# Turning the differential keys through VectorE's squares and DRAM, and moving their scores

## The reference

```python
proj = jnp.einsum('bsd,dn->bsn', rms_norm(x, pre_w, NORM_EPS), w_in)
dq, dk, dv, dg, sq, sk, sv, sg, iq, ik, iw = jnp.split(proj, SPLIT_OFFSETS, axis=-1)
dq = apply_rope(dq.reshape(b, s, DIFF_HEADS, 2, DIFF_QK_DIM), cos_d, sin_d)
dk = apply_rope(dk.reshape(b, s, DIFF_HEADS, 2, DIFF_QK_DIM), cos_d, sin_d)
# differential attention, causal:
p = softmax(einsum('bqhcd,bkhcd->bhcqk', dq, dk) * scale)
oa = einsum('bhqk,bkhe->bqhe', p[:, :, 0] - lam * p[:, :, 1], dv)
# sparse attention: top 64 causal keys of sum_h relu(iq_h . ik) * iw_h
ob = softmax(einsum(sq, sk_chosen) * scale) @ sv_chosen
mix = concatenate([rms_norm(oa, subln_w) * (1 - lambda_init) * silu(dg), ob * silu(sg)])
out = x + rms_norm(mix @ w_out, post_w)
```

## Time and profile before

| | |
|---|---|
| Median of 3 runs | 300.79 us (300.02 to 301.07) |
| The profiled execution | 299.94 us, its span 298.1 us |
| TensorE matmuls | 291.0 us (98%) |
| TensorE weight loads | 245.5 us (82%) |
| VectorE | 235.9 us (79%) |
| ScalarE | 163.9 us (55%) |
| GpSimd | 70.1 us (24%) |
| DMA | 61.05 MB, 205 GB/s over the span |
| Granted TensorE clock | 0.994 of full |

### The profile page before, as it was taken

One profiled execution on the slowest core, in us unless ns is written; L12 is line 12 of the kernel. 1 busy time (PEld: TensorE's weight loads), 2 busy tenths in 40 slices (PEclk: granted clock), 3 DMA queues, 4 the chain that ended last, 5 costly groups with the idle time before them and its releaser, 6 DMA issues.

```text
span 298.1 us, 4395 instructions
## 1 busy us (share of the span) xinstructions
PE 291.0 (98%) x1560; PEld 245.5 (82%) x1560; DVE 235.9 (79%) x476; ACT 163.9 (55%) x284; POOL 70.1 (24%) x116
## 2 busy tenths in 40 slices
PE   8999999999999999999999999999999999999992
PEld 7799778788787888888888988778888788888892
DVE  4853989889999996966984686978999999878543
ACT  5976863736577473803665854473737756391101
POOL 6548510203030311101070740002303030310101
PEclk9999999999999999999999999999999999999997
DMA  7999959467528669981059799937644684746012
GB/s 262 373 369 386 366 217 347 133 158 222 184 89 184 239 178 286 253 243 48 0 158 372 245 350 243 305 143 202 219 141 143 117 305 146 183 86 154 1 70 70
DMA packets 66741, 61.05 MB, mean 205 GB/s; under 512 B 38816, under 2 KB 43680, under 8 KB 66720
## 3 DMA queue, kind: packets, MB, share of 16 engines
q1 hardware_dynamic: 66432, 60.52, 65.0%
q10 hardware_dynamic: 288, 0.26, 0.3%
HBM read 55.01 MB, written 5.77 MB: 204 GB/s over the span
## 4 chain that ended last, share of the span: by engine, by line
PE 94%; DMA 2%; SPq 1%; ACT 0%; DVE 0%; issue 0%; POOLq 0%; DVEq 0%; POOL 0%; ACTq 0%
PE bank_a L469 20%; PE bank_a L478 20%; PE bank_a L474 20%; PE bank_a L626 7%; PE bank_s L626 6%; PE bank_o L603 4%; PE bank_t L448 3%; DMA w_raw<-in_w_in 2%; PE bank_a L486 2%; PE bank_s L587 2%; PE bank_s L579 1%; PE bank_s L567 1%; PE bank_t L626 1%; PE bank_o L474 1%; PE bank_s L474 1%; PE bank_o L478 1%
## 5 line engine op out<-in xcount | busy, mean ns | idle before, releaser
L994 DVE TENSOR_TENSOR w_lo<-w_raw,w_hi 128x2048 fp32r<-128x2048 f32 (+1 forms) x46 | 98.5, 2147 | 17.9 <-ACT w_hi L770 17.6
L770 ACT ACTIVATE w_hi<-w_raw 128x2048 fp32r<-128x2048 f32 (+1 forms) x46 | 81.9, 1785 | 31.5 <-PE bank_a L478 23.3
L469 PE MATMUL bank_a<-w_hi,h_hi 128*128 128x512 f32 (+1 forms) x272 | 72.4, 388 | 0.0
L478 PE MATMUL bank_a<-w_lo,h_hi 128*128 128x512 f32 (+1 forms) x272 | 70.0, 379 | 0.0
L474 PE MATMUL bank_a<-w_hi,h_lo 128*128 128x512 f32 (+1 forms) x272 | 69.9, 379 | 0.0
L478 PEld LDWEIGHTS bank_a<-w_lo,h_hi 128*128 128x128 f32 x272 | 49.6, 188 | 10.1 <-DVE w_lo L994 0.7
L474 PEld LDWEIGHTS bank_a<-w_hi,h_lo 128*128 128x128 f32 x272 | 49.8, 188 | 9.8
L469 PEld LDWEIGHTS bank_a<-w_hi,h_hi 128*128 128x128 f32 x272 | 48.0, 188 | 10.4 <-issue 2.7
L838 ACT ACTIVATE xt_pbuf<-xt_pbuf,st 128x128 f32<-128x128 f32 (+1 forms) x48 | 21.3, 444 | 25.1 <-DVE st L1143 25.1
L1437 POOL TENSOR_TENSOR rt<-nat,tab 128x256 f32<-128x256 f32 x10 | 7.4, 740 | 112.2 <-ACT nat L822 112.1
L822 ACT ACTIVATE nat<-bank_a,st 128x512 f32<-128x512 f32 x20 | 13.5, 681 | 19.6 <-PE bank_a L478 19.6
(11 more groups left out here) (199 smaller groups left out, 430.8 us busy)
## 6 DMA issues: line engine op xcount, KB each, us to landing
w_raw<-in_w_in SPq DMA_DIRECT2D x30, 1024.0 KB, 5.9
w_raw<-in_w_out SPq DMA_DIRECT2D x8, 1024.0 KB, 6.0
w_raw<-in_w_in SPq DMA_DIRECT2D x8, 584.0 KB, 7.4
turned<-mixn SPq DMA_DIRECT2D x20, 128.0 KB, 2.7
prm<-in_rows SPq DMA_DIRECT2D x2, 705.0 KB, 6.9
w_raw<-in_w_in SPq DMA_DIRECT2D x2, 512.0 KB, 6.4
xres<-in_x SPq DMA_DIRECT2D x2, 512.0 KB, 9.9
dqT<-turned SPq DMA_DIRECT2D x2, 512.0 KB, 5.9
```

The lines of the kernel that those rows point to most:

```text
L469: pe.matmul(bank, h_hi[:, HALF * half + kk, tok], whi[:, kk, :], start=half == 0 and kk == 0, stop=False)
L478: mm = pe.matmul(bank, h_hi[:, HALF * half + kk, tok], wlo[:, kk, :], start=False, stop=half == 1 and kk == HALF - 1)
L770: act.activation(unit(w_hi, u), unit(raw, u), ACT.Copy).then_inc(hi_done.sem, 1)
L994: dve.tensor_tensor(unit(w_lo, u), unit(raw, u), unit(w_hi, u).bitcast(F32), ALU.subtract).then_inc(lo_done.sem, 1)
```

## The change

Differential keys take the way through VectorE's squares and DRAM as the queries do. TensorE's eight transposes and VectorE's two copies a layer go; a turning of squares, four puts and two readings come, with semaphores dk_squares, dk_put and dk_landed and one more DRAM buffer. The scores 6 to 9 stand half a chunk later in TensorE's list, behind second(14), and 10 and 11 behind second(15). The turnings of probabilities and VectorE's and ScalarE's lists are arranged around that. The copy of the index keys stands ahead of split_lo(9) in layer 0. On SP some readings and puts stand one weight unit earlier (index queries, PS1, the mixture), and the parameters' reading two units later.

```diff
-T_IK, T_DK, T_PD0, T_PD1A, T_SK, T_PD1B = 4, 5, 7, 8, 9, 11
+T_IK, T_PD0, T_PD1A, T_SK, T_PD1B = 4, 5, 6, 7, 9
...
@@ SP
                     if layer and u == 8:
                         sp.wait_ge(iq_squares, 1)
                         put(0, squares, iq_put)
-                    if layer and u == 9:
                         sp.wait_ge(iq_put, 16 * SQUARES)
                         get(0, iqT, iq_landed)
...
+                    if u == 14:
+                        sp.wait_ge(dk_squares.sem, dk_squares.at(layer, 1))
+                        put(DKS, squares, dk_put.sem)
+                        sp.wait_ge(dk_put.sem, dk_put.at(layer, 16 * SQUARES))
+                        for b in range(BLOCKS):
+                            sp.dma_start(dkT[:, :, b * P:(b + 1) * P], scratch[DKS][:, b * HEADS:(b + 1) * HEADS, :]).then_inc(dk_landed.sem, 16)
...
-                    if layer == 0 and u == 1:
+                    if layer == 0 and u == 3:
                         sp.dma_start(prm[:, :], rows[0:1, :].to_broadcast([P, ROW_N])).then_inc(prm_landed.sem, 16)
...
                     if u == 1:
                         get_probs(layer, PS0)
-                    if u == 2:
                         put_probs(layer, PS1)
...
                         get_probs(layer, PS1)
-                    if u == 3:
+                    if u == 2:
                         sp.wait_ge(mix_put.sem, mix_put.at(layer, 16 * SQUARES))
@@ TensorE
-                turn_nat(T_DK, 0, 3)
                 first(13)
-
-                pe.wait_ge(t_drained.sem, t_drained.at(layer, T_DK + 2))
-                pe.wait_ge(dq_landed.sem, dq_landed.at(layer, dq_landed.per_layer))
-                diff_scores(6, 0, range(HEADS))
-                diff_scores(8, 1, (0, 1))
                 second(13)
                 first(14)
                 second(14)
+
+                pe.wait_ge(dq_landed.sem, dq_landed.at(layer, dq_landed.per_layer))
+                pe.wait_ge(dk_landed.sem, dk_landed.at(layer, dk_landed.per_layer))
+                diff_scores(6, 0, range(HEADS))
+                diff_scores(8, 1, (0, 1))
                 first(15)
+                second(15)
+                diff_scores(10, 1, (2, 3))
+                first(16)
 
                 pe.wait_ge(combined.sem, combined.at(layer, 1))
                 turn_probs(T_PD0, 6, 0, HEADS)
-                diff_scores(10, 1, (2, 3))
-                second(15)
 
                 pe.wait_ge(combined.sem, combined.at(layer, 2))
                 turn_probs(T_PD1A, 8, 1, 2)
-                first(16)
                 second(16)
                 turn_nat(T_SK, 0, 5)
                 first(17)
 
-                pe.wait_ge(combined.sem, combined.at(layer, 3))
-                turn_probs(T_PD1B, 10, 1, 2)
-
                 pe.wait_ge(t_drained.sem, t_drained.at(layer, T_SK + 2))
                 pe.wait_ge(sq_landed.sem, sq_landed.at(layer, sq_landed.per_layer))
                 dsa_scores(12, 0, range(HEADS))
+
+                pe.wait_ge(combined.sem, combined.at(layer, 3))
+                turn_probs(T_PD1B, 10, 1, 2)
@@ ScalarE
                 split_hi(layer, 16)
+                move(13)
+                move(14)
                 exps(6, 0, 4)
                 exps(7, 0, 4)
-                move(13)
                 split_hi(layer, 17)
                 exps(8, 1, 2)
                 exps(9, 1, 2)
-                move(14)
+                move(15)
                 split_hi(layer, 18)
                 exps(10, 1, 2)
                 exps(11, 1, 2)
-                move(15)
@@ VectorE
+                if layer == 0:
+                    drain(T_IK, ikT[:, :])
                 split_lo(layer, 9)
-                drain(T_IK, ikT[:, :])
+                if layer:
+                    drain(T_IK, ikT[:, :])
...
                 mask_unchosen(0)
+                dve.wait_ge(dq_put.sem, dq_put.at(layer, 16 * SQUARES))
+                turn_squares(0, 3, dk_squares.sem)
                 split_lo(layer, 14)
 
-                choose(1, 1)
-                drain_pair(T_DK, dkT)
+                choose(1, 3)
+                split_lo(layer, 15)
                 choose(1, 2)
-                split_lo(layer, 15)
+                split_lo(layer, 16)
                 mask_scores(6, 0, 4, causal[:, P:SEQ])
                 mask_scores(7, 0, 4, causal[:, P:SEQ])
-                choose(1, 2)
+                mask_scores(8, 1, 2, causal[:, :])
+                mask_scores(9, 1, 2, causal[:, :])
...
                 combine(6, 0, HEADS, 0)
 
-                mask_scores(8, 1, 2, causal[:, :])
-                mask_scores(9, 1, 2, causal[:, :])
-                dve.wait_ge(dq_put.sem, dq_put.at(layer, 16 * SQUARES))
+                dve.wait_ge(dk_put.sem, dk_put.at(layer, 16 * SQUARES))
                 turn_squares(1, 4, sq_squares.sem)
-                split_lo(layer, 16)
                 combine(8, 1, 2, 0)
-
+                split_lo(layer, 17)
+                choose(1, 2)
                 drain(T_PD0, pT[:, 0, :])
                 mask_scores(10, 1, 2, causal[:, :])
                 mask_scores(11, 1, 2, causal[:, :])
-                split_lo(layer, 17)
-                choose(1, 2)
                 drain(T_PD1A, pT[:, 1, :])
+                choose(1, 1)
+                drain_pair(T_SK, skT)
                 combine(10, 1, 2, 2)
-                choose(1, 1)
+                split_lo(layer, 18)
+                mask_scores(12, 0, 4, work[0][:, :])
+                drain(T_PD1B, pT[:, 2, :])
                 mask_unchosen(1)
-                drain_pair(T_SK, skT)
-                split_lo(layer, 18)
-
-                drain(T_PD1B, pT[:, 2, :])
-                mask_scores(12, 0, 4, work[0][:, :])
+                turn_probs(PS0, 12)
                 split_lo(layer, 19)
-                turn_probs(PS0, 12)
-                split_lo(layer, 20)
-
-                gate_diff(0)
-                split_lo(layer, 21)
                 mask_scores(13, 1, 2, work[1][:, :])
                 mask_scores(14, 1, 2, work[1][:, :])
 
+                gate_diff(0)
+                split_lo(layer, 20)
                 turn_probs(PS1, 14)
                 dve.wait_ge(subln_ready.sem, subln_ready.at(layer, 1))
-                drain_mix(T_MD0, m_hi, m_lo, 0, subln)
                 gate_diff(1)
                 turn_mix()
+                drain_mix(T_MD0, m_hi, m_lo, 0, subln)
+                split_lo(layer, 21)
```

More of the change, by code:

```diff
@@ L86 @@
 ROW_N = sum(ROW.values())
-T_IK, T_DK, T_PD0, T_PD1A, T_SK, T_PD1B = 4, 5, 7, 8, 9, 11
-T_MD0, T_MS0, T_MS1 = 12, 13, 14
-T_USES = 15
-PS0, MD1S, PS1 = range(3, 6)
+T_IK, T_PD0, T_PD1A, T_SK, T_PD1B = 4, 5, 6, 7, 9
+T_MD0, T_MS0, T_MS1 = 10, 11, 12
+T_USES = 13
+DKS, PS0, MD1S, PS1 = range(3, 7)
 LANES = 32
@@ L236, in build_trunk @@
         iq_squares, iq_landed = sem("iq_squares"), sem("iq_landed")
+        dk_squares, dk_put, dk_landed = count("dk_squares", 1), count("dk_put", 16 * SQUARES), count("dk_landed", 16 * BLOCKS)
         dq_squares, sq_squares = count("dq_squares", 1), count("sq_squares", 1)
@@ L820, in move @@
                         act.wait_ge(dq_squares.sem, dq_squares.at(layer, 1))
+                    if chunk == SK:
+                        act.wait_ge(dk_squares.sem, dk_squares.at(layer, 1))
                     root = {DQ: rd, SQ: rs}.get(chunk, rx)
```

## The result

The changed kernel takes 304.49 us (median of 6 runs, 304.13 to 305.90) beside 300.42 us for the kernel before (6 runs, 299.95 to 301.07): a ratio of 1.0141, 95% interval 1.0117 to 1.0165. It is slower by 4.1 us. Two later runs in a slower state, one of the kernel before (367.93 us) and one of the third experiment (979.17 us), are in none of the medians. The profiled execution took 304.84 us, its span 303.1 us, 5.0 more than the 298.1 of before.

A forecast was written before the change was run, and what follows sets the result against it. TensorE's back-to-back list was taken as the bound: 299.94 + 2 x (2.6 - 0.97) - 0.2 + 0.1 = 303.1 us profiled; from the runs' median, 300.79 + 3.2 = 304.0 us, range 301.2 to 307.2.

The forecast's parts named there:

- TensorE's list: TensorE's sequence of work: without the eight differential-key transposes it is 0.97 us a layer ahead if nothing makes it wait.
- The wait at SK: Value-key transposes wait for VectorE's copies of PD0 and PD1A: 2.6 us a layer, about 1.1 and 1.5.
- The one loose term: Ahead of PD1A's copy, one VectorE product and split_lo(17) each wait for GpSimd's rotary work: 1.0 us, bounds 0 and 2.4.
- Rival 1: No wait at SK, PD1A being copied before 99.33: 298.7 us, chance 0.1.
- all 14.5 us of VectorE's work: VectorE's work between the first mask and PD1A's copy, without a wait; TensorE is there 14.5 us later.
- What is late next: With the wait for PD1A gone, the drain of SK behind it would still come late; no size given.
- The keys through DRAM: Differential keys' readings, issued at 77.1 and 77.5, land between 80 and 83.4, taken as 81.5, needed at 83.67: no wait.
- The opening: Parameters' reading behind unit 7 lets units 6 and 7 land up to 2 us earlier: 0.2 us gained, bounds 0 and 0.5.
- PS0: Layer 0: reading of PS0's probabilities comes behind the next layer's unit 0: 0.1 us added, bounds 0 and 0.5.
- rival 5: TensorE's clock falls to 1.2 GHz in the new pause: 2.7 us more a layer, 309 us, chance 0.05.
- the base: Starting time of the forecast: median of the runs, 300.79 us, with the profiled execution 0.85 below it.

The follow-up runs named there:

- third experiment: Changed kernel with GpSimd's rope of the value-side keys SK left out but for one head's columns of one block: 301.3 us, ratio 1.0034.
- reordered kernel: Changed kernel with only VectorE's list rearranged: copies of PD0 and PD1A behind split_lo(17), two rounds of choose moved behind PD1B's copy: 298.75 us, ratio 0.9951.
- last one: Reordered kernel with the reading of PS0's probabilities directly behind their puts, ahead of the next layer's unit 0: 298.75 us.
- first experiment: Changed kernel with VectorE's copies of PD0 and PD1A right behind split_lo(17), ahead of two rounds of choose and masks 10 and 11: 301.94 us, ratio 1.0060.
- second experiment: The run of the reordered kernel, against the changed kernel: 298.75 us, ratio 0.9951.
- late reading alone: Kernel before with only the parameters' reading moved behind unit 7 in layer 0: 299.85 us, ratio 0.9989.
- pause filled: Changed kernel with unread 512-column matmuls, three ahead of the first four value-key transposes and four ahead of the second four: 302.94 us, ratio 1.0087.
- fifth kernel: Changed kernel with the parameters' reading put back behind unit 5: 305.32 us (303.91 to 306.48, 5 runs).

## Why the prediction came out right, and where only the sum did

**TensorE's list**: 0.97 us a layer predicted, 0.92 measured, in layer 1 of the reordered kernel and in layer 0 of the last one. Eight transposes and one interruption, nothing hidden.

**The wait at SK**: mechanism, place and size are as walked. In layer 0, with the predicted value in brackets: from the first mask (84.71) to combine(6) 4.27 us (4.27); combine(8) starts at 92.7 (92.8); PD1A's copy ends at 101.6 (101.9); waits of 1.10 and 1.47 (1.1 and 1.5). The one loose term was GpSimd, at 0.74 for 1.0, inside the bounds of 0 and 2.4. Two of VectorE's instructions met it, as supposed, but neither was held for a whole one of GpSimd's: the products took 0.49 more and the low half 0.26. In the changed kernel no mask and no bank copy ran beside the rope of SK. Elsewhere copies did, untouched: in before PD1A's copy took 0.69 us beside GpSimd's last instruction (98.77 to 99.51, its usual 0.74), and in the first experiment both copies together took 1.27 us beside the rope and 1.29 for a pair away from it.

The Trainium skill (GPSIMD Engine Reference, Key points) has GpSimd contend with VectorE's instructions that have two SBUF inputs or run in a two-port mode, and the copies fit that. No mask ran beside the rope in any of the kept traces, so of the masks they show nothing.

**Rival 1** rested on the sentence that "even an ideal order only breaks even". That holds only as long as all 14.5 us of VectorE's work stay ahead of the copy. The second experiment puts some of it behind, and both copies are out at 98.4, before TensorE asks (98.78). So the wait was a choice of order.

**What is late next**: said of the case without the wait for PD1A, and shown by the first experiment: the drain of SK, 1.56 us late.

**The keys through DRAM**: their readings were issued at 76.90 (77.1 predicted) and landed 3.2 us later, as the page's list of DMA issues has it:

```profile
dkT<-turned SPq DMA_DIRECT2D x4, 256.0 KB, 3.2
```

They were in at about 80.5, 3 us ahead of the scores: the early end of my range, and not the 81.5 that I took. The rule of the Trainium skill on 512-byte pieces (DMA: Bandwidth & Descriptors, Specifications) had pointed to that end, and the trace agrees.

**The opening**: 0.2 us predicted, bounds 0 and 0.5; 0.4 measured, with the late reading alone and from before to after (18.68 to 18.28). The mechanism is right (ScalarE's high copies of units 6 and 7 start 1.7 and 2.1 us earlier in after), the term was too small. I took a part of the weight loads' waits of 0.7 us; more than half of them came back, and without the late reading a low half that is just in time in before is late in the changed kernel.

**PS0**: 0.1 us predicted in layer 0, and 0.1 lost there. It is no more because the pause has made TensorE late itself; with the pause gone it loses 0.5 (second experiment). The cover was the very wait that I had added elsewhere.

**The clock, rival 5**: this is the step that failed. I gave it 0.05 and argued that pauses of 1.1 and 1.5 us are shorter than the 2 us after the last matmul in the earlier trace rows. That took one row for a limit, and took the two pauses one by one, though TensorE works only 0.41 us between them. In the profiled execution the clock fell in one layer of two. The other executions can be read by their mean granted clock. With the pause filled it is 0.995 to 0.998. Of after's six, five have 0.992 or 0.993, and the slowest (305.90 us) 0.986. Of the fifth kernel's five, the fastest (303.91) has 0.996, three (305.19 to 305.36) 0.990 to 0.992, and the slowest (306.48) 0.987. Steps of 1.1 to 1.4 us are near what no fall, one and two would give. So I take it that the clock falls in one of the layers in most executions and in none or both in some; only the two profiled ones, with one fall each, show it in a timeline. I had priced it at 2.7 a layer, a whole half group more; it lasts 3.4 us in which TensorE works on at half speed, and costs 1.6.

**The total**: 304.0 forecast, 304.49 measured, and the closeness is partly luck. With the clock kept the changed kernel takes 302.9, so my sum without the clock was about 1.1 too high. Of that, 0.4 to 0.5 is the base: I had added the 0.85 us between the profiled execution and the median of three (300.79), and more runs put that median at 300.4 and 300.2. The opening gave 0.2 more than I allowed. The other 0.4 or so stays open; medians of 4 to 6 runs don't settle it. The clock, which the sum left out, took 1.55. The sign doesn't hang on it: with the clock kept the ratio is 1.0087, still slower.

## What to carry to other kernels

When an edit renumbers or moves the users of a shared buffer, ask for each of them whose release it waits for, and what stands ahead of that release on the other engine. Here the change shortened the busy engine's list by 1.8 us and lost 5.1 at a bank whose copy stood behind selection and masks that nobody was waiting for; with those moved behind the copies the same change gains 1.5. A pause of the matmul engine is priced twice, once for its length and once for the clock that it may cost.

## What the runs showed of the hardware

- TensorE's granted clock fell to 0.50 at the end of a pause of 1.1 and 1.5 us with four transposes between. In the fifth kernel it fell 0.9 us after TensorE had gone on (at 103.2, the pause over at 102.3), again for 3.4 us. It did so in one layer of the two in both profiled executions; what decides it, no run shows. In the eight executions with one wait of about 1.5 us and a short one of 0.4 a layer (first and third experiments) the mean clock is 0.994 to 0.998, so that no such loss is seen. After the last matmul it held for about 2.0 us in before, and for about 4 in after (columns as in the earlier trace rows):

```profile
297.00:298.00 1.00, 0.43 (x4) 0.22 (x2) 0.03 (x1) 0.47 (x2) 0.00 (x0) 1.00 0.00 0
...
300.00:301.00 1.00, 0.00 (x0) 0.00 (x0) 0.57 (x2) 0.00 (x0) 0.00 (x0) 1.00 0.37 139
301.00:302.00 1.00, 0.00 (x0) 0.00 (x0) 0.00 (x0) 0.00 (x0) 0.00 (x0) 0.77 0.99 346
```

So one row at the end of a trace is no limit for what a pause may be.

- Where GpSimd's rope ran beside VectorE's products and low halves, both lost time in places, and not evenly. Of the rope of SK beside VectorE's low half, one of two like instructions took 2.39 us and the other 0.53 (0.46 in before), while VectorE's lost 0.26:

```profile
94.37 0.53 POOL L1445 TENSOR_TENSOR rt<-nat,tab 128x128 f32<-128x128 f32 x1
94.98 2.39 POOL L1446 TENSOR_TENSOR rt<-nat,tab 128x128 f32<-128x128 f32 x1
```

In the earlier trace rows it is the other way round: VectorE's products lose 1.6 us and GpSimd's first instruction nothing.
